# Retention states of two heads side by side with zeros, and earlier loads of three tensors

## The chip, the cores and the metric

One NeuronCore of a Trainium2 chip runs the whole program. The metric is the device time in microseconds (us) of one launch, median of the runs shown. TensorE (PE), VectorE (DVE), ScalarE (ACT), GpSimd (POOL) and the DMA queues of SyncE (SP), ACT and POOL are programmed by hand and meet at semaphores.

## The reference, cut to what matters

A two-layer decoder trunk, 1024 tokens by 1024 columns, float32. Layer 0 normalises x and multiplies it by one weight matrix of 3352 columns. Columns 0 to 2047 are queries, keys, values and a gate of 8 retention heads of width 64; columns 2048 to 2559 are the queries of 8 sparse-attention heads, and the rest their keys, values and gates. Retention works on chunks of 128 tokens:

```python
scores = einsum('bhcid,bhcjd->bhcij', q_c, k_c) * decay
y_intra = einsum('bhcij,bhcje->bhcie', scores, v_c)
chunk_kv = einsum('bhcjd,bhcje->cbhde', k_c * k_decay, v_c)
state = chunk_decay * state + kv          # one 64 x 64 state a head
y_inter = einsum('bhcid,cbhde->bhcie', q_c * q_decay, prev_states)
y = y_intra + y_inter                     # then a norm per head and a gate
```

Sparse attention, an output projection and a mixture of 32 experts (two of them per token) follow. Layer 1 has a gated convolution in place of the attention, and another mixture of experts. Each expert mixture adds two weighted rows per token to the residual stream.

## The kernel before, in words

`project_and_retain` computes the projection in 7 column blocks (six of 512 columns and one of 280), each for 8 tiles of 128 tokens. A product of one block and one tile is 24 matmuls (line 511): 8 slices of the depth, in three parts (high by high, high by low, low by high) that together give float32 accuracy. Each result goes through `stage` to the tensor `proj` in memory.

Retention is put in between. From block 3 (`GATE`) on, `step(b, t)` gives each chunk of 128 tokens four products in a row; after the first of them comes TURN, after the second SCORE, after the third WEIGH. So 8 chunks fill blocks 3 to 6, and the last WEIGH stands after the product of block 6, tile 6, with one product behind it.

- TURN (`turn_queries`, line 520): 8 transposes of queries and keys into `ps_a`.
- SCORE (`score`): the scores of each head, keys by queries with depth 64 (line 530), from partitions 0 to 63 for even heads (`a` = 0) and 64 to 127 for odd ones (`a` = 1), into two banks of `ps_s`; then each head's own key-value product (line 537) with 64 columns of output partitions, in the lower or upper half of `ps_kv`. A float32 matmul of these shapes is two instructions in the trace. The order is all four heads of `a` = 0, then all four of `a` = 1.
- WEIGH (`weigh`): for each head, scores by values with depth 128 (line 548), then decayed queries by `state` with depth 64 (line 550), accumulated in the same 64 columns of `ps_a`. The two kinds alternate, 16 matmuls in all.

The state of heads 2b and 2b+1 stands in partitions 0 to 63 and 64 to 127 of `state[:, b, :]`. ACT takes the result of WEIGH (lines 362 and 363), DVE updates `state` (lines 442 and 444) and norms and gates the rows in `norm_weighed`, POOL's queue stores them to `mixer`.

`rows_of_heads` is the next stage. Its block starts when every engine has ended the projection's. SP's queue then loads the queries of tile 0, all keys (two loads), two gains, `q_rows`, the queries of tiles 1 to 7, then the keys and values of the other branches. ACT and DVE wait for the keys, gains and `q_rows` together (`keys_loaded`), then work tile by tile. The queries `nq` lie where the projection's raw weights `raw` lay.

`experts` is the mixture. It ends with the last expert's output scattered to `slots` by a POOL DMA (line 1192). DVE sets `finished` when the last split of weights is done, and SP then loads tiles 0 to 3 of the residual rows for the stage that follows (`NextRows.load`, line 1069) while the last expert ends.

Two stages follow a mixture. `mix_and_conv` loads from `slots` two rows per token and tile (`ya`, line 1460, four tiles ahead), then residual rows of tiles 4 to 7, then the first convolution weights (line 1472, split by ACT at line 1514 and DVE at line 1568, in order between the tiles' work). `finish` loads `ya` of all 8 tiles and, after those of each tile from 4 on, its residual rows; DVE adds them up (line 2587), ACT's queue stores the output.

Of the kernel before, what the change touches and what calls it, by code (L numbers as in the profile page):

```python
# [16 lines left out]
ALU = mybir.AluOpType  # L17
# [173 lines left out]
def project_and_retain(nc, name, src, gain, w, width, out, ret_gain, con, y_out, cst, region):  # L191
# [8 lines left out]
    VALUES, GATE = 2, 3  # L200
    with Pool_(nc, name) as m:
# [20 lines left out]
        state = m.sb("state", [P, PAIRS, HD])  # L222
# [7 lines left out]
        ps_y = ps_a[:].rearrange("p a b n -> p a (b n)")  # L230
# [26 lines left out]
        with nc.Block(no_gpsimd_drain=True) as block:  # L257
            @block.sync
            def _(sp):
# [18 lines left out]
                for b in range(1, n_blocks):  # L278
                    for c in range(2):
                        load_weights(b, c)  # L280
                for s in range(4):
                    sp.wait_ge(stage_stored[s], 16 * n_blocks * (NT // 4))
# [38 lines left out]
            def _(act):  # L321
# [35 lines left out]
                def take_weighed(c):  # L357
                    act.wait_ge(y_ready, c + 1)
                    if c >= 2:
                        act.wait_ge(y_stored[c % 2], 16 * (c // 2))  # L360
                    halves = ps_y[:, :, 0:PAIRS * HD].rearrange("p a (b d) -> p a b d", d=HD)
                    act.activation(y_sq.rearrange("p (b a d) -> p a b d", a=2, d=HD), halves, ACT.Square)
                    act.activation(y[:, c % 2, :].rearrange("p (b a d) -> p a b d", a=2, d=HD), halves, ACT.Copy
                                   ).then_inc(y_taken, 1)
# [34 lines left out]
            def _(dve):  # L399
# [39 lines left out]
                def norm_weighed(c):  # L439
                    dve.wait_ge(kv_ready, c + 1)  # L440
                    dve.wait_ge(y_ready, c + 1)
                    dve.tensor_tensor(state[:], state[:], c_decay[:].unsqueeze(2).to_broadcast([P, PAIRS, HD]), ALU.mult)
                    dve.drain()
                    dve.tensor_tensor(state[:], state[:], ps_kv[:, 0:PAIRS, :], ALU.add).then_inc(state_ready, 1)
# [48 lines left out]
            def _(pe):  # L493
# [30 lines left out]
                def score(c):  # L524
                    pe.wait_ge(T_ready, c + 1)
                    pe.wait_ge(decayed, c)
                    for a in range(2):
                        at = slice(a * HD, (a + 1) * HD)
                        for b in range(PAIRS):
                            last = pe.matmul(ps_s[:, a, b, :], qkT[at, 1, b, :], qkT[at, 0, b, :], start=True, stop=True)  # L530
# [3 lines left out]
                    for a in range(2):  # L534
                        for b in range(PAIRS):
# [5 lines left out]
                def weigh(c):  # L541
                    pe.wait_ge(qd_ready, c + 1)
                    pe.wait_ge(decayed, c + 1)
                    for a in range(2):
                        at = slice(a * HD, (a + 1) * HD)
                        for b in range(PAIRS):
                            h = 2 * b + a
# [513 lines left out]
class NextRows:  # L1061
# [5 lines left out]
    def load(self, sp, tiles):  # L1067
        for t in tiles:
# [3 lines left out]
def experts(nc, name, data, lists, slots, most, ident, following):  # L1072
# [14 lines left out]
    with Pool_(nc, name) as m:  # L1087
# [59 lines left out]
        with nc.Block(no_gpsimd_drain=True) as block:  # L1147
            @block.sync
            def _(sp):
# [28 lines left out]
                following.load(sp, range(NT // 2))  # L1178
# [237 lines left out]
def mix_and_conv(nc, name, ahead_rows, slots, gates, gain, mix_out, cst, w, conv_w, conv_b, zT_hi, zT_lo, z_places, ahead, region):  # L1416
# [5 lines left out]
    with Pool_(nc, name) as m:  # L1422
# [31 lines left out]
        with nc.Block() as block:  # L1454
            @block.sync
            def _(sp):
# [13 lines left out]
                ahead_rows.load(sp, range(NT // 2, NT))  # L1470
# [207 lines left out]
def rows_of_heads(nc, name, proj, q_gain, k_gains, cst, con, keep, region):  # L1678
# [4 lines left out]
    with Pool_(nc, name) as m:  # L1683
        nq, kv, kvc = region.head_rows()
# [9 lines left out]
        rows_loaded, keys_loaded, pool_loaded, rest_loaded, mask_loaded = (  # L1694
            m.sems("rows_loaded", NT), m.sem("keys_loaded"), m.sem("pool_loaded"), m.sem("rest_loaded"), m.sem("mask_loaded"))
# [5 lines left out]
        with nc.Block() as block:  # L1701
            @block.sync
            def _(sp):
                def load_queries(t):
                    sp.dma_start(nq[:, t, :], proj[t * P:(t + 1) * P, C_NQ:C_KC]).then_inc(rows_loaded[t], 16)

                load_queries(0)
# [5 lines left out]
                for t in range(1, NT):  # L1713
                    load_queries(t)
# [764 lines left out]
def trunk(nc, a, con, out):  # L2479
# [3 lines left out]
    with ctx:  # L2483
# [10 lines left out]
        with Pool_(nc, "all", whole=True) as top:  # L2494
# [23 lines left out]

            with Pool_(nc, "in") as m:
# [111 lines left out]
```

## Time and profile before

| | us |
|---|---|
| median of 3 runs (2167.07 to 2169.96) | 2167.11 |
| profiled execution, its own time | 2173.11 |
| its span, first to last instruction | 2171.4 |
| projection with retention, until the next stage's first load | 418.0 |
| TensorE busy in the span | 1873.8 |

The profile is of one execution. The page lists costly groups of instructions; the trace answers finer questions: what one engine ran in a few microseconds (the timeline), how busy each engine was in a stretch and which clock TensorE was granted (windows), who waited for whom (waits). Matmuls overlap in the pipeline, so the time from one start to the next says more than the duration of one.

### The profile page before, as it was taken

The page shows a single profiled execution, that of the slowest core. Times are in us where ns is not written, and L with a number is a line of the kernel's source. Part 1 is how long each engine was busy: PE and PEld are TensorE (multiplying, and loading weights), DVE is VectorE, ACT ScalarE, POOL GpSimd, SP SyncE. Part 2 cuts the span into 40 slices and gives each one's busy share as a digit, 9 for nine tenths or more (in the row PEclk, how much of TensorE's full clock was granted, in tenths as well). Part 3 has the DMA queues.
Part 4 walks back from the last instruction along what each step waited for, and adds up shares of the span by engine and source line. Part 5 has one row for each costly group of instructions (what it writes and reads, how often), then busy time and mean ns, then how long its engine had stood idle before and what let it go on. Part 6 is the DMA issues. An engine that isn't in the chain of part 4 may idle for free. (4 is left out here: it accounts for less than half of the span.)

```text
span 2171.4 us, 25604 instructions
## 1 busy us (share of the span) xinstructions
PE 1873.8 (86%) x9608; PEld 1548.8 (71%) x9608; DVE 1223.7 (56%) x1566; ACT 865.5 (40%) x928; POOL 317.4 (15%) x258
## 2 busy tenths in 40 slices
PE   8999999655789999986999992799999959999980
PEld 7888888645577788865888772688887847888760
DVE  5223322366555544565999883633324557999873
ACT  4111221231233333234888882311112126888860
POOL 0000000000110000111443420000000112434420
PEclk9999889685799999987999996899999978999995
DMA  5333212340200003455999966521124348999947
GB/s 199 127 117 107 99 57 78 117 95 1 78 1 1 1 1 104 167 190 230 362 381 372 367 269 224 173 58 50 39 65 164 135 178 325 381 381 372 373 161 296
DMA packets 145297, 374.40 MB, mean 172 GB/s; under 512 B 40078, under 2 KB 75150, under 8 KB 120446
## 3 DMA queue, kind: packets, MB, share of 16 engines
q1 hardware_dynamic: 113542, 309.54, 38.9%
q0 software_dynamic: 22432, 45.53, 5.8%
q10 hardware_dynamic: 9216, 17.93, 2.2%
q8 instruction: 63, 1.03, 0.2%
q14 instruction: 44, 0.36, 0.1%
HBM read 331.38 MB, written 75.10 MB: 187 GB/s over the span
## 5 line engine op out<-in xcount | busy, mean ns | idle before, releaser
L1242 PE MATMUL ex_ps_h<-even_split 128*128 128x512 f32 x768 | 195.9, 406 | 9.2 <-DVE even_split L1356 9.0
L1242 PE MATMUL ex_ps_h<-odd_split 128*128 128x512 f32 x768 | 196.0, 406 | 8.9 <-DVE odd_split L1356 8.5
L511 PE MATMUL in_ps<-in_w_hi,in_xT_hi 128*128 128x512 f32 (+1 forms) x448 | 179.1, 400 | 1.7 <-DVE in_xT_lo L416 1.7
L1242 PEld LDWEIGHTS ex_ps_h<-even_split 128*128 128x128 f32 x768 | 142.5, 192 | 48.7 <-DVE even_split L1356 14.9
L1242 PEld LDWEIGHTS ex_ps_h<-odd_split 128*128 128x128 f32 x768 | 142.5, 192 | 48.4 <-DVE odd_split L1356 15.3
L511 PE MATMUL in_ps<-in_w_lo,in_xT_hi 128*128 128x512 f32 (+1 forms) x448 | 175.0, 391 | 0.0
L511 PE MATMUL in_ps<-in_w_hi,in_xT_lo 128*128 128x512 f32 (+1 forms) x448 | 174.3, 389 | 0.0
L1630 PE MATMUL conv_ps<-conv_xT_hi,conv_w_hi 128*128 128x512 f32 x384 | 150.4, 392 | 0.9 <-DVE conv_w_lo L1568 0.9
L1630 PE MATMUL conv_ps<-conv_xT_lo,conv_w_hi 128*128 128x512 f32 x384 | 149.8, 390 | 0.0
L1630 PE MATMUL conv_ps<-conv_xT_hi,conv_w_lo 128*128 128x512 f32 x384 | 149.7, 390 | 0.0
L2333 ACT ACTIVATE att_prob<-att_ps_s 128x512 f32<-128x512 f32 x114 | 67.9, 597 | 175.3 <-PE att_ps_s L2271 175.1
L423 DVE COPY in_stage<-in_ps 128x512 f32<-128x512 f32 (+1 forms) x56 | 36.7, 656 | 176.9 <-PE in_ps L511 176.9
L2285 PE MATMUL att_ps_o<-mix_v,att_prob 128*128 128x128 f32 x912 | 125.9, 284 | 0.3 <-DVE even_attended L2393 0.3
L2285 PEld LDWEIGHTS att_ps_o<-mix_v,att_prob 128*128 128x128 f32 x912 | 122.4, 201 | 4.6 <-ACT att_prob L2333 0.7
L2361 DVE TENSOR_REDUCE att_low<-att_ps_m 128x2 f32<-128x768 f32 (+7 forms) x80 | 71.8, 916 | 68.7 <-PE att_ps_m L2236 67.0
L511 PEld LDWEIGHTS in_ps<-in_w_hi,in_xT_hi 128*128 128x128 f32 x448 | 89.3, 199 | 19.0 <-DVE in_xT_lo L416 2.1
L511 PEld LDWEIGHTS in_ps<-in_w_hi,in_xT_lo 128*128 128x128 f32 x448 | 89.0, 199 | 16.3
L511 PEld LDWEIGHTS in_ps<-in_w_lo,in_xT_hi 128*128 128x128 f32 x448 | 89.5, 200 | 15.3
L1263 PE MATMUL ex_ps_y<-even_split,ex_h_hi 128*128 128x512 f32 x256 | 83.6, 408 | 5.4 <-DVE ex_h_lo L1370 5.4
L1263 PE MATMUL ex_ps_y<-odd_split,ex_h_hi 128*128 128x512 f32 x256 | 83.5, 408 | 5.4 <-DVE ex_h_lo L1370 5.4
L1630 PEld LDWEIGHTS conv_ps<-conv_xT_hi,conv_w_hi 128*128 128x128 f32 x384 | 72.4, 189 | 16.3 <-DVE conv_w_lo L1568 1.3
L990 PE MATMUL out_ps_o<-even_split,even_x_hi 128*128 128x512 f32 x256 | 81.6, 400 | 2.5 <-DVE even_x_lo L925 2.5
(343 smaller groups left out, 4060.9 us busy)
## 6 DMA issues: line engine op xcount, KB each, us to landing
all_region<-in_moe_w_gate SPq DMA_DIRECT2D x16, 1024.0 KB
all_region<-in_moe_w_up SPq DMA_DIRECT2D x16, 1024.0 KB
all_region<-in_moe_w_down SPq DMA_DIRECT2D x16, 1024.0 KB
experts_w_gu<-in_moe_w_gate SPq DMA_DIRECT2D x16, 1024.0 KB
experts_w_gu<-in_moe_w_up SPq DMA_DIRECT2D x16, 1024.0 KB
experts_w_d<-in_moe_w_down SPq DMA_DIRECT2D x16, 1024.0 KB, 15.0
all_region<-in_ev_w_in SPq DMA_DIRECT2D x12, 1024.0 KB, 7.5
proj<-in_stage ACTq DMA_DIRECT2D x48, 256.0 KB, 2.0
```

The lines of the kernel that those rows point to most:

```text
L423: dve.tensor_copy(stage[:, q % 4, 0:n], ps[:, q % BANKS, 0:n]).then_inc(staged, 1)
L511: last = pe.matmul(ps[:, q % BANKS, 0:n], a[:, k, at], w_part[:, b % 2, k, 0:n], start=(k == 0 and j == 0), stop=(k == KT - 1 and j == 2))
L990: last = pe.matmul(ps_o[:, t % 2, cols], a[:, k, :], w_part[:, b, k, :], start=(k == 0 and j == 0), stop=(k == KT - 1 and j == 2))
L1242: last = pe.matmul(ps_h[:, u % 2, :], a[:, u % 2, k, :], w[:, k, :], start=(k == 0 and j == 0), stop=(k == KT - 1 and j == 2))
L1263: last = pe.matmul(ps_y[:, at], a[:, u % 2, k, :], w[:, k, at], start=(k == 0 and j == 0), stop=(k == DE // P - 1 and j == 2))
L1630: last = pe.matmul(ps[:, j, at], w_part[:, j, k, :], x_part[:, k, at], start=(k == 0 and q == 0), stop=(k == KT - 1 and q == 2))
L2285: last = pe.matmul(ps_o[:, b, h * P:(h + 1) * P], prob[:, c % 4, h * P:(h + 1) * P], keep.v_all[:, v_at:v_at + P], start=(j == first_tile( ...
L2333: act.activation(prob[:, c % 4, :], ps_s[:, c % 2, :], ACT.Exp).then_inc(exped, 1)
L2361: dve.tensor_reduce(low[:, n % 2, b, hs[0]:hs[-1] + 1], src, X, ALU.max, negate=True).then_inc(reduced, 1)
```

## The change

The state is kept as `[P, PAIRS, 2, HD]`: for a pair of heads b, partitions 0 to 63 hold the even head's state in columns 0 to 63 and zeros in 64 to 127, partitions 64 to 127 zeros and then the odd head's state. One product of depth 128 and 128 columns then gives both heads' second term. WEIGH does its 8 products of scores and values first, then 4 of these, all in one bank. DVE updates the two halves apart. SCORE's loops are turned round, so that even and odd heads alternate. The sparse heads' queries are loaded by SP's queue in the projection, once their rows are in memory and the last raw weights are split. Residual rows of all 8 tiles are loaded when the experts' last split is done.

```diff
-        state = m.sb("state", [P, PAIRS, HD])
+        state = m.sb("state", [P, PAIRS, 2, HD])
-        ps_y = ps_a[:].rearrange("p a b n -> p a (b n)")
+        ps_y = ps_a[:, 0, :, :].rearrange("p b n -> p (b n)")
...
+                for c in range(2):
+                    sp.wait_ge(lo_ready[c], n_blocks)
+                for t in range(NT):
+                    in_memory(sp, QUERIES, t)
+                    ahead.load_queries(sp, t)
...
-                    halves = ps_y[:, :, 0:PAIRS * HD].rearrange("p a (b d) -> p a b d", d=HD)
-                    act.activation(y_sq.rearrange("p (b a d) -> p a b d", a=2, d=HD), halves, ACT.Square)
-                    act.activation(y[:, c % 2, :].rearrange("p (b a d) -> p a b d", a=2, d=HD), halves, ACT.Copy
-                                   ).then_inc(y_taken, 1)
+                    act.activation(y_sq, ps_y, ACT.Square)
+                    act.activation(y[:, c % 2, :], ps_y, ACT.Copy).then_inc(y_taken, 1)
...
-                    dve.tensor_tensor(state[:], state[:], c_decay[:].unsqueeze(2).to_broadcast([P, PAIRS, HD]), ALU.mult)
-                    dve.drain()
-                    dve.tensor_tensor(state[:], state[:], ps_kv[:, 0:PAIRS, :], ALU.add).then_inc(state_ready, 1)
+                    halves = [(slice(a * HD, (a + 1) * HD), a) for a in range(2)]
+                    for at, a in halves:
+                        dve.tensor_tensor(state[at, :, a, :], state[at, :, a, :],
+                                          c_decay[at, :].unsqueeze(2).to_broadcast([HD, PAIRS, HD]), ALU.mult)
+                    dve.drain()
+                    for at, a in halves:
+                        last = dve.tensor_tensor(state[at, :, a, :], state[at, :, a, :], ps_kv[at, 0:PAIRS, :], ALU.add)
+                    last.then_inc(state_ready, 1)
...
-                    for a in range(2):
-                        at = slice(a * HD, (a + 1) * HD)
-                        for b in range(PAIRS):
+                    for b in range(PAIRS):
+                        for a in range(2):
+                            at = slice(a * HD, (a + 1) * HD)
                             last = pe.matmul(ps_s[:, a, b, :], qkT[at, 1, b, :], qkT[at, 0, b, :], start=True, stop=True)
...
-                    for a in range(2):
-                        for b in range(PAIRS):
+                    for b in range(PAIRS):
+                        for a in range(2):
                             h = 2 * b + a
                             last = pe.matmul(ps_kv[a * HD:(a + 1) * HD, b, :], kd[:, h * HD:(h + 1) * HD],
...
-                            pe.matmul(ps_y[:, a, b * HD:(b + 1) * HD], scores[:, a, b, :],
-                                      qkv[:, c % 2, 2 * RET_W + h * HD:2 * RET_W + (h + 1) * HD], start=True, stop=False)
-                            last = pe.matmul(ps_y[:, a, b * HD:(b + 1) * HD], qdT[at, b, :], state[at, b, :],
-                                             start=False, stop=True)
+                    for h in range(RH):
+                        pe.matmul(ps_y[:, h * HD:(h + 1) * HD], scores[:, h % 2, h // 2, :],
+                                  qkv[:, c % 2, 2 * RET_W + h * HD:2 * RET_W + (h + 1) * HD],
+                                  start=(h == 0), stop=False, skip_group_check=True)
+                    for b in range(PAIRS):
+                        last = pe.matmul(ps_y[:, b * P:(b + 1) * P], qdT[:, b, :],
+                                         state[:, b, :, :].rearrange("p a d -> p (a d)"),
+                                         start=False, stop=(b == PAIRS - 1), skip_group_check=True)
...
-                following.load(sp, range(NT // 2))
+                following.load(sp)
...
-                ahead_rows.load(sp, range(NT // 2, NT))
...
+class HeadRows:
+    def load_queries(self, sp, t):
+        sp.dma_start(self.nq[:, t, :], self.proj[t * P:(t + 1) * P, C_NQ:C_KC]).then_inc(self.loaded[t], 16)
...
-                load_queries(0)
...
-                for t in range(1, NT):
-                    load_queries(t)
...
-                    if t >= NT // 2:
-                        ahead_rows.load(sp, [t])
```

## Rows read from the trace of the kernel before

**Rows 1.** The page: TensorE's granted clock in 40 slices of the span, tenths.

```profile
PEclk9999889685799999987999996899999978999995
```

**Rows 2.** Windows, one chunk of retention each; busy us (instructions), then clock and DMA.

```profile
164.90:199.18 34.28, 34.28 (x172) 28.14 (x169) 13.39 (x18) 5.61 (x7) 2.69 (x5) 0.90 0.44 146
...
368.07:392.72 24.65, 24.65 (x172) 22.92 (x169) 7.96 (x15) 5.61 (x7) 0.54 (x1) 0.86 0.10 35
```

**Rows 3.** Timeline of TensorE's matmuls in the first chunk: start, us, what.

```profile
164.10 1.03 PE L520 MATMUL in_ps_a<-all_ident,all_region 128*128 128x128 f32 x8
...
170.52 1.71 PE L530 MATMUL in_ps_s<-in_xn 64*128 64x128 f32 x16
172.16 0.97 PE L537 MATMUL in_ps_kv<-all_region,in_xin 128*64 128x64 f32 x16
173.05 0.50 PE L511 MATMUL in_ps<-in_w_hi,in_xT_hi 128*128 128x512 f32 x1
...
178.63 0.33 PE L548 MATMUL in_ps_a<-all_region,in_xin 128*128 128x64 f32 x2
178.89 0.43 PE L550 MATMUL in_ps_a<-in_state,in_xn 64*128 64x64 f32 x2
179.25 0.43 PE L548 MATMUL in_ps_a<-all_region,in_xin 128*128 128x64 f32 x2
...
182.90 0.69 PE L548 MATMUL in_ps_a<-all_region,in_xin 128*128 128x64 f32 x2
...
185.37 0.79 PE L511 MATMUL in_ps<-in_w_hi,in_xT_hi 128*128 128x512 f32 x1
```

**Rows 4.** Windows in SCORE, TensorE alone: busy us (matmuls in flight), clock.

```profile
170.88:170.92 0.04, 0.04 (x3) 1.00 0.00 0
...
171.44:171.48 0.04, 0.04 (x6) 1.00 0.00 0
```

**Rows 5.** Windows on line 1904 (first) and line 1997, both TensorE: busy, clock.

```profile
483.30:488.00 4.70, 4.62 (x42) 4.43 (x40) 1.00 0.00 0
...
510.00:520.00 10.00, 9.34 (x45) 9.73 (x44) 0.50 0.01 2
```

**Rows 6.** Timeline from the last WEIGH to the next stage, all engines.

```profile
401.67 0.33 PE L548 MATMUL in_ps_a<-all_region,in_xin 128*128 128x64 f32 x2
...
409.25 0.60 PE L511 MATMUL in_ps<-in_w_hi,in_xT_hi 128*128 128x280 f32 x1
...
409.43 0.43 DVE L442 TENSOR_TENSOR in_state<-in_state,in_c_decay 128x256 f32<-128x256 f32 x1 [7.11 <-PE in_ps_a L550]
...
415.65 0.33 ACTq L344 DMA_DIRECT2D proj<-in_stage  x1
418.00 0.34 SPq L1705 DMA_DIRECT2D all_region<-proj  x1
```

**Rows 7.** Waits in `rows_of_heads`: us in total, times, longest.

```profile
ACT heads_n_sq L1754 <- DMA heads_q_rows<-con_q_rows: 15.7, 1, 15.7
```

**Rows 8.** The end: timeline of the last scatter and `finish`, two windows, a wait.

```profile
2113.25 1.76 SPq L1069 DMA_DIRECT2D all_region<-stream  x4
...
2120.30 0.97 POOL L1192 DMA_INDIRECT slots<-ex_y,odd_idx  x1 [9.96 <-ACT ex_y L1317]
2127.60 5.56 SPq L2577 DMA_DIRECT2D end_ya<-slots  x10
...
2120.40:2123.60 3.20, 0.00 (x0) 0.00 (x0) 0.00 (x0) 0.00 (x0) 0.87 (x1) 0.68 0.19 68
...
2149.40:2164.50 15.10, 0.00 (x0) 0.00 (x0) 7.70 (x7) 0.00 (x0) 0.00 (x0) 0.50 1.01 410
...
DVE all_region L2587 <- DMA all_region<-stream: 10.9, 4, 3.7
```

**Rows 9.** Waits at the start of `mix_and_conv`: us in total, times, longest.

```profile
DVE all_region L1547 <- DMA odd_zT_lo_again<-slots: 7.9, 2, 4.7
ACT conv_w_hi L1514 <- DMA odd_zT_hi_again<-in_od_w_in: 4.9, 1, 4.9
```

More of the change, by code:

```diff
@@ L188, in load, with project_and_retain @@
             sp.dma_start(self.raw[b][:, at, :], self.w_k[:, at, b * COLS:(b + 1) * COLS]).then_inc(self.loaded[2 * b + c], 16)
-def project_and_retain(nc, name, src, gain, w, width, out, ret_gain, con, y_out, cst, region):
+def project_and_retain(nc, name, src, gain, w, width, out, ret_gain, con, y_out, cst, region, ahead):
     n_blocks = -(-width // COLS)
@@ L199, in project_and_retain @@
     PAIRS = RH // 2
-    VALUES, GATE = 2, 3
+    VALUES, GATE, QUERIES = 2, 3, 4
     with Pool_(nc, name) as m:
@@ L543, in weigh @@
                     pe.wait_ge(decayed, c + 1)
[L544 to L547, printed above, removed]
-                            pe.matmul(ps_y[:, a, b * HD:(b + 1) * HD], scores[:, a, b, :],
-                                      qkv[:, c % 2, 2 * RET_W + h * HD:2 * RET_W + (h + 1) * HD], start=True, stop=False)
-                            last = pe.matmul(ps_y[:, a, b * HD:(b + 1) * HD], qdT[at, b, :], state[at, b, :],
-                                             start=False, stop=True)
+                    for h in range(RH):
[6 more added lines that the diff above has]
+                                         start=False, stop=(b == PAIRS - 1), skip_group_check=True)
                     last.then_inc(y_ready, 1)
@@ L1065, in __init__, with load @@
         self.src, self.rows, self.loaded = src, region.stream_rows(), m.sems(name, NT)
-    def load(self, sp, tiles):
-        for t in tiles:
+    def load(self, sp):
+        for t in range(NT):
             sp.dma_start(self.rows[:, t, :], self.src[t * P:(t + 1) * P, :]).then_inc(self.loaded[t], 16)
@@ L1675, with __init__, rows_of_heads @@
 KEY_EXT = EXT + 2 * R
-def rows_of_heads(nc, name, proj, q_gain, k_gains, cst, con, keep, region):
+class HeadRows:
+    def __init__(self, m, proj, region):
+        self.proj, self.loaded = proj, m.sems("head_rows_loaded", NT)
+        self.nq, self.kv, self.kvc = region.head_rows()
+    def load_queries(self, sp, t):
+        sp.dma_start(self.nq[:, t, :], self.proj[t * P:(t + 1) * P, C_NQ:C_KC]).then_inc(self.loaded[t], 16)
+def rows_of_heads(nc, name, proj, q_gain, k_gains, cst, con, keep, ahead):
     NK = 2 * G
@@ L1683, in rows_of_heads @@
     with Pool_(nc, name) as m:
-        nq, kv, kvc = region.head_rows()
+        nq, kv, kvc = ahead.nq, ahead.kv, ahead.kvc
         gains = m.sb("gains", [P, 3, HD])
@@ L1693, in rows_of_heads @@
         ps_n = m.ps("ps_n", [P, 3, ROUND, P])
-        rows_loaded, keys_loaded, pool_loaded, rest_loaded, mask_loaded = (
-            m.sems("rows_loaded", NT), m.sem("keys_loaded"), m.sem("pool_loaded"), m.sem("rest_loaded"), m.sem("mask_loaded"))
+        rows_loaded = ahead.loaded
+        keys_loaded, pool_loaded, rest_loaded, mask_loaded = (
+            m.sem(n) for n in ("keys_loaded", "pool_loaded", "rest_loaded", "mask_loaded"))
         eps_ready, n_squared, n_summed, n_rooted, rows_added, n_ready = (
@@ L1703, in _ @@
             def _(sp):
-                def load_queries(t):
-                    sp.dma_start(nq[:, t, :], proj[t * P:(t + 1) * P, C_NQ:C_KC]).then_inc(rows_loaded[t], 16)
-                load_queries(0)
                 for j, (a, b) in enumerate(((C_KS, C_VS), (C_KW, C_VW))):
@@ L2517, in route @@
                                   data, lists, rows)
+            head_rows = HeadRows(top, proj, region)
             with Pool_(nc, "in") as m:
                 project_and_retain(nc, "in0", a["x"][0, :, :], a["mix_norm_g"][0, :], a["ev_w_in"][0, :, :], IN_W, proj,
-                                   a["ev_ret_norm_g"][0, :], con, mixer, cst, region)
+                                   a["ev_ret_norm_g"][0, :], con, mixer, cst, region, head_rows)
             with Pool_(nc, "even") as held:
@@ L2531, in trunk @@
                             rows_of_heads(nc, "heads", proj, a["ev_q_norm_g"][0, :], a["ev_k_norm_g"][0, :, :], cst, con, keep,
-                                          region)
+                                          head_rows)
                             sparse_prepare(nc, "prep", a["ev_q_norm_g"][0, :], a["ev_k_norm_g"][0, :, :], a["ev_cmp_pe"][0, :, :, :],
```

## The prediction

> **What bounds the kernel now.** I read the page first, for the clock. TensorE runs at 2.4 GHz when the granted clock is 1.0 and at 1.2 GHz when it is 0.5; a slice that shows 8 or 9 tenths mixes the two levels [rows 1]. The projection fills the first 418 us. Windows cut along the chunks show TensorE busy for all of each, at a mean clock of 0.90, falling to 0.86 where the products are narrow, while DVE has 13.4 us of work in 34.3, ACT 5.6 and POOL 2.7 [rows 2]. So in this stage every microsecond of TensorE is one of the kernel, until the last WEIGH; DVE, ACT and DMA follow.
>
> The timeline shows what retention costs between the products [rows 3]. TURN's eight transposes are short. SCORE runs from 170.52 to 173.05, 2.53 us. WEIGH runs from 178.63 to 185.37, 6.74 us, for 32 instructions. At 182.90 a pair's duration jumps from 0.43 to 0.69 us: the clock has gone to half, inside WEIGH and nowhere else in the chunk. The chunk's mean of 0.90 says for how long: 0.1 of 34.28 us is lost, so 6.8 us ran at half clock. The last two products of this chunk carry the rest of it. The next TURN comes 34.28 us after 164.10, at 198.38, so those two take 13.01 us, where one at full clock takes 5.58 (173.05 to 178.63). The narrower chunk shows the same loss (0.14 of 24.65 us is 3.45), so it is one such stretch a chunk.
>
> Why is WEIGH slow before the fall? The two kinds alternate every 0.36 us, two instructions each (178.89 to 179.25), 0.18 us an instruction. A stream of one kind with 128 columns of weights goes faster: 42 instructions of line 1904 in 4.70 us, 0.112 each, at full clock [rows 5]; two of them would take 0.22. So each change between 128 and 64 rows of depth costs about 0.14 us, and there are 16 of them in a WEIGH.
>
> **The change, part by part.**
>
> WEIGH. 32 instructions in 16 alternating pairs become 24 of one depth: 16 with 64 columns and 8 with 128, all with 128 columns of weights. At 0.112 [rows 5] that is 2.7 us, and there is no change of depth left within it or at its edges. Per chunk 6.74 − 2.7 = 4.0 us go. If the clock then does not fall, the two products behind it take 11.1 instead of 13.0, another 1.9. That makes 5.9 us for each of 7 chunks, 41.3 us. The bounds of an instruction are 0.055 (line 537's 16 in 0.89 us, with half the weight columns) and 0.21 (line 1997, 45 in 9.34 us at half clock [rows 5]): WEIGH between 1.3 and 5.0 us. I take 0.112, because the shape of line 1904 is the one nearest, 128 by 128. The zeros cost nothing more: the product has 128 columns for two heads, where it had 64 for each.
>
> The last chunk. Its WEIGH took 7.58 us, 401.67 to 409.25 [rows 6], and takes 2.7: 4.9 less. From 409.25 to 418.00 are 8.75 us more, 6.4 until the last store's issue at 415.65 and 2.35 for it to land. At full clock the last product would end some 2 us sooner. But in DVE's order the whole norm of the weighed rows, which begins with line 442 at 409.43, stands ahead of the copy of that product, and it gets longer by two state operations of 0.43 [rows 6]. So between nothing and 2 us go here; I take 0.4, near the lower end, since the norm's chain over DVE and ACT sets the copy from now on. The last chunk gives 5.3 in all.
>
> DVE. Two more state operations a chunk, at most 0.43 us each, since the elements a partition are as before. In the other chunks they hide under the products: DVE is idle over 20 us of 34 [rows 2]. If that cover were gone they would cost 7 us over the eight chunks. ACT reads the same 512 elements in one stretch: nothing. The longer clear of `state` lies before the first x tile is in.
>
> SCORE. Even and odd heads now alternate. In the old order one half alone keeps 3 matmuls in flight, and at 171.44 there are 6 [rows 4]: the second half started before the first was done, so the two halves do run side by side. Eight instructions of one half at 0.11 are 0.9 us, plus an edge of 0.2, against 1.64 (170.52 to 172.16), so 0.5 less if both start together. Line 537 likewise: 16 in 0.89 us, one half 0.44 and an edge of 0.15, so 0.3 less. That is 0.8 a chunk, 6.4 us. From below the bound is nothing gained, from above 8 × 1.2 = 10 (half of 2.53 each); the loss that it could bring is a rival below. The Trainium skill, page "TensorEngine Tiling (Array Packing)", section "Key Properties", says that a change of tiling mode drains the engine, but not a change of tile, and that different tiles can load weights and multiply in parallel. By that rule WEIGH loses its pauses and SCORE gains none; the trace agrees with the first part by its 0.14 us and with the second by the six in flight.
>
> Queries ahead. Eight loads of 256 KB move to SP's queue in the projection, behind the last weights. Nothing of the stage stands behind them on that queue but waits for stores that come later anyway, and the DMA engines are busy for 0.44 of the time or less in these chunks [rows 2]. In `rows_of_heads` ACT starts after a wait that `q_rows` ended [rows 7]. One query load stood ahead of it (0.34 us of issue [rows 6], 256 KB) and seven right behind it shared the engines. The bounds are that issue alone and all 2.1 MB at 410 GB/s [rows 8], 5.1 us; I take 1.5, near the lower one, because only one of the eight stood ahead. Later the stage goes by DVE and ACT tile by tile, so that other loads land sooner buys nothing.
>
> Residual rows, at the end. In `finish` DVE waited 10.9 us over four tiles for rows of the stream; from 2149.4 to 2164.5 the DMA engines moved 410 GB/s at full share [rows 8]. Four loads of 512 KB less are 2.1 MB, 5.2 us at that rate. They now go right behind the first four, which were issued from 2113.25 on. The scatter was issued at 2120.30 and moved 68 GB/s for 3.2 us, 0.2 MB, and the last stage began at 2127.60. Eight loads at 410 GB/s take 10.2 us, to about 2124: ahead of 2127.6, but across the scatter. I give 1 us back for it: 4.2, bounds 1 and 5.2. DVE's own work there, two operations of 1.3 us a tile, is 21 us, so DMA stays the limit.
>
> Residual rows, after the first mixture. The same four loads stood ahead of the first convolution weights, for which ACT waited 4.9 us, with the next tile's squares behind it in ACT's order and the split behind it in DVE's [rows 9]. 2.1 MB less ahead of the weights is 5.1 us and takes the 4.9 away. Less 1 for the scatter and 0.4 because DVE comes to its part of the weights later than ACT: 3.5. Bounds are 1, and 6 if some of DVE's 7.9 us for the gathered rows [rows 9] goes too.
>
> **The sum.** 41.3 + 5.3 + 6.4 + 1.5 + 4.2 + 3.5 = 62.2 us. The profiled execution took 2173.11 (span 2171.4 and 1.7 around it), so the same would show 2110.9 for it. It lies 6.0 above the median of the runs; from 2167.11 the forecast is 2104.9, say 2105. A run tells differences from about 0.2%, 4.3 us, here.
>
> **Rivals.**
>
> The clock still falls in each WEIGH. For it: line 1997, 128 columns of weights by 64 columns, the shape of the new WEIGH's first 16 instructions, ran at 0.50 without a rise while TensorE was over 90% busy [rows 5]. Against it: those 16 are 1.8 us, the 8 behind them have line 1904's shape, which was at 1.0, and SCORE, 2.5 us long and about as light, shows no fall in any chunk. Price: 6.8 us at half clock lose 3.4, eight times 27: 2132. Chance 0.13.
>
> Alternating halves pause. If each of the 14 changes of half in SCORE costs the 0.14 us of a change of depth, that is 2.0 a chunk, 16 us, and the 6.4 are not gained: 2127. The six in flight speak against it. Chance 0.10.
>
> The same on the other side: this is also what could make the kernel slower. It decides when one of the 8 × 14 changes of half costs more than (62.2 − 6.4) / 112 = 0.50 us, three and a half times the pause in WEIGH. At 0.6 the time would be 2105 + 6.4 + 67 = 2179. Chance 0.02.
>
> The moved rows gain nothing: eight loads delay the last scatter, and the next stage starts as much later as it gets shorter. For it: the scatter's data has the engines to itself today [rows 8]. Against: it is only 0.2 MB. Price 7.7: 2113. Chance 0.12. The Trainium skill, page "DMA: Bandwidth & Descriptors", section "Issuing engines are not separate DMA queues", says that transfers of all engines' queues interleave on the same 16; by that the scatter shares rather than waits its turn, and this rival would cost about 1 to 2 us instead. No row here has the two together.
>
> The forecast itself, with its terms within their bounds, has 0.60, and 0.03 is left to what I do not see.
>
> **How the numbers follow.** The likeliest case's own range: 2096 if WEIGH is 2.4 us, SCORE gains 10 and the row loads all of their 5 to 6; 2114 if SCORE gains nothing and the heads and row loads little. The pause in SCORE reaches 2127 and the moved rows 2113. Leaving out most of the clock's case at 2132, the slow case and a little below, the range is 2094 to 2130. Slower by over 0.2% needs the 0.50 us pause or something unseen: 0.02. Within 0.2%: 0.02. Faster: 0.96.
>
> **What would show it.** In the profile after: one chunk in 34.3 − 5.9 − 0.8 = 27.6 us; no 0.50 stretch in blocks 3 to 6, a mean clock of 1.00 there; WEIGH near 2.7 us with no pauses; SCORE near 1.7; the next stage's first load near 365; the first squares of the heads about 1.5 us sooner after it; no wait of DVE for rows of the stream in `finish`, and its length down from 44 to 39 us. The prediction is wrong if the clock row still shows 0.9 in the chunks, if instructions of WEIGH stay at 0.18 us because what slows them is the accumulation into columns just written and not the change of depth, or if the stages behind the mixtures start late.

## The result and the profile after

The changed kernel takes 2116.94 us (median of 4 runs, 2111.78 to 2119.13), against 2168.45 (4 runs, 2167.07 to 2169.96) for the one before on the same chip: a ratio of 0.9759, 95% interval 0.9739 to 0.9779, 51.5 us in the medians. Three later measurements of the same two kernels gave 59.1, 59.0 and 57.2 us. The forecast was 2105, in a range of 2094 to 2130, with a change of 62.2.

The profiled execution took 2111.78 us (span 2110.2), 61.3 less than the profiled one of before. It is the fastest of its four; the other three have spans of 2114.7 to 2117.5 at a mean granted clock of 0.913 to 0.916 where it has 0.919. The profiled one of before was slower than all four of its runs in that comparison. So the stage comparisons below flatter the change, by some 10 us in all against the first medians and by 2 to 4 against the later ones, and the medians are the better measure of the whole.

The clock row of the page after, 40 slices of the span:

```profile
PEclk9999999767899999969999995999999969999995
```

The nearly eight slices of the projection [rows 1] are now nearly seven, and the two 8s among their 9s are gone. A slice does not show a stretch of 6.8 us, so I cut windows along the chunks again; one chunk to a line, busy us (instructions) of PE, PEld, DVE, ACT, POOL, then clock, DMA share and GB/s. The last line is the wide middle of the narrow last block.

```profile
163.03:190.33 27.30, 27.30 (x162) 22.97 (x161) 14.24 (x18) 5.62 (x7) 2.70 (x5) 1.00 0.55 183
190.33:217.63 27.30, 27.30 (x162) 22.97 (x161) 9.83 (x16) 9.33 (x9) 1.61 (x3) 1.00 0.26 87
320.00:344.00 24.00, 24.00 (x206) 23.40 (x205) 11.93 (x21) 6.20 (x8) 1.62 (x3) 1.00 0.21 70
```

A chunk takes 27.30 us, where it took 34.28 at a clock of 0.90 [rows 2]. The clock is 1.00 throughout. TensorE is still busy for all of it, so it is still what bounds the stage. The timeline of TensorE in the first chunk:

```profile
163.03 1.03 PE L530 MATMUL in_ps_a<-all_ident,all_region 128*128 128x128 f32 x8
...
169.44 1.16 PE L540 MATMUL in_ps_s<-in_xn 64*128 64x128 f32 x16
170.54 0.69 PE L547 MATMUL in_ps_kv<-all_region,in_xin 128*64 128x64 f32 x16
171.15 0.50 PE L521 MATMUL in_ps<-in_w_hi,in_xT_hi 128*128 128x512 f32 x1
...
176.75 1.89 PE L556 MATMUL in_ps_a<-all_region,in_xin 128*128 128x64 f32 x16
178.48 1.11 PE L560 MATMUL in_ps_a<-in_state,in_xn 128*128 128x128 f32 x8
179.34 0.48 PE L521 MATMUL in_ps<-in_w_hi,in_xT_hi 128*128 128x512 f32 x1
...
351.23 1.89 PE L556 MATMUL in_ps_a<-all_region,in_xin 128*128 128x64 f32 x16
352.96 1.11 PE L560 MATMUL in_ps_a<-in_state,in_xn 128*128 128x128 f32 x8
353.83 0.37 PE L521 MATMUL in_ps<-in_w_hi,in_xT_hi 128*128 128x280 f32 x1
```

SCORE goes from 169.44 to 171.15, 1.71 us for 2.53 [rows 3]. WEIGH goes from 176.75 to 179.34, 2.59 us for 6.74, in two rows in place of sixteen pairs, because no idle time cuts them apart. The last chunk's WEIGH is the same, 2.60 for 7.58 [rows 6]. What follows it, all engines but TensorE:

```profile
359.41 0.45 DVE L428 COPY in_stage<-in_ps 128x280 f32<-128x280 f32 x1
359.68 0.55 POOL L321 DMA_DIRECT2D mixer<-in_y  x1 [17.18 <-DVE in_y L466]
359.89 0.33 ACTq L351 DMA_DIRECT2D proj<-in_stage  x1
363.53 1.00 SPq L1727 DMA_DIRECT2D all_region<-proj  x2
```

The copy now ends DVE's chain right behind the norm, as the prediction read it from the order. The two last stores are issued within 0.3 us of each other (1.5 apart before), and the stage ends 3.64 us after the last, for 2.35. From the end of the last WEIGH to the next stage are 9.7 us, for 8.75. All of the increase is behind the last store's issue: up to it are 6.06 us, for 6.40. In the thirteen profiles of kernels with the change or most of it, the stage ends 3.35 to 3.78 us after that issue.

The stage behind, and the two places where the rows of the stream moved:

```profile
372.91 0.63 ACT L1770 ACTIVATE heads_n_sq<-all_region 128x512 f32<-128x512 f32 x1 [15.30 <-DMA heads_q_rows<-con_q_rows]
...
1256.94 4.25 SPq L1080 DMA_DIRECT2D all_region<-stream  x8
...
1264.13 0.97 POOL L1203 DMA_INDIRECT slots<-ex_y,even_idx  x1 [10.09 <-ACT ex_y L1328]
1276.74 0.80 SPq L1471 DMA_DIRECT2D odd_zT_lo_again<-slots  x2
...
2052.53 6.79 SPq L1080 DMA_DIRECT2D all_region<-stream  x8
2059.71 0.98 POOL L1203 DMA_INDIRECT slots<-ex_y,odd_idx  x1 [10.08 <-ACT ex_y L1328]
2072.53 10.83 SPq L2594 DMA_DIRECT2D end_ya<-slots  x16
```

After the last scatter of the second mixture the kernel now waits 12.8 us for the last stage to begin, where it waited 7.3 [rows 8]; after the first mixture 12.6, where it was 9.25 (1321.62 to 1330.87). Windows from the issue to just before the first packet of the scatter, and from there to its last, by the trace's records of packets:

```profile
2059.80:2064.00 4.20, 0.00 (x0) 0.00 (x0) 0.00 (x0) 0.00 (x0) 0.89 (x1) 0.68 1.03 376
2064.10:2068.10 4.00, 0.00 (x0) 0.00 (x0) 0.00 (x0) 0.00 (x0) 0.00 (x0) 0.50 0.58 226
```

While the rows of the stream fill the engines (share 1.03), no packet of the scatter moves. Its first starts 4.4 us after the issue, where it took 1.5 before (2120.30 to 2121.84), and its packets spread over 4.0 us, where they took 1.6.

The stages against before; heads and the convolution each from its first load to the next stage's first:

| | before | after | difference | forecast |
|---|---|---|---|---|
| projection, to the first load of the next stage | 418.00 | 363.53 | −54.5 | −53.0 |
| heads | 44.2 | 41.9 | −2.3 | −1.5 |
| last scatter of the first mixture to the convolution | 9.25 | 12.6 | +3.4 | +1 |
| the convolution's stage | 314.8 | 311.1 | −3.7 | −4.5 |
| last scatter of the second mixture to `finish` | 7.3 | 12.8 | +5.5 | +1 |
| `finish`, to the end of the span | 43.8 | 37.7 | −6.1 | −5.2 |

They add up to −57.7 of the −61.2 between the spans; the other 3.5 lie in stages that the change does not touch. Of the 54.5, 1.1 stand ahead of the first chunk (its TURN starts at 163.03 for 164.10), where nothing was changed; the other profiles have that start anywhere from 162.8 to 164.2.

### The profile page after: what moved, and what is told of

It reads as the page before. It is cut to its first block and busy times, and to the rows that moved or that the text cites. A ratio compares the mean times of both kernels' runs of the same rounds, so it can differ in the third digit from the quotient of the medians.

```text
span 2110.2 us, 25493 instructions
## 1 busy us (share of the span) xinstructions
PE 1815.4 (86%) x9544; PEld 1504.2 (71%) x9544; DVE 1231.0 (58%) x1582; ACT 865.2 (41%) x928; POOL 317.4 (15%) x258
## 3 DMA queue, kind: packets, MB, share of 16 engines
q1 hardware_dynamic: 113542, 309.54, 39.9%
## 5 line engine op out<-in xcount | busy, mean ns | idle before, releaser
L521 PE MATMUL in_ps<-in_w_hi,in_xT_hi 128*128 128x512 f32 (+1 forms) x448 | 171.8, 384 | 1.7 <-DVE in_xT_lo L421 1.7
L521 PE MATMUL in_ps<-in_w_lo,in_xT_hi 128*128 128x512 f32 (+1 forms) x448 | 168.9, 377 | 0.0
L521 PE MATMUL in_ps<-in_w_hi,in_xT_lo 128*128 128x512 f32 (+1 forms) x448 | 168.8, 377 | 0.0
L521 PEld LDWEIGHTS in_ps<-in_w_hi,in_xT_hi 128*128 128x128 f32 x448 | 84.7, 189 | 17.1 <-DVE in_xT_lo L421 2.1
L521 PEld LDWEIGHTS in_ps<-in_w_hi,in_xT_lo 128*128 128x128 f32 x448 | 84.6, 189 | 15.3
L521 PEld LDWEIGHTS in_ps<-in_w_lo,in_xT_hi 128*128 128x128 f32 x448 | 84.7, 189 | 14.3
```

Of the source, the lines that this page charges most:

```text
L521: last = pe.matmul(ps[:, q % BANKS, 0:n], a[:, k, at], w_part[:, b % 2, k, 0:n], start=(k == 0 and j == 0), stop=(k == KT - 1 and j == 2))
```

## The experiments

Every kernel here computes all of the reference. The changed kernel itself ran again as the control three times, each time beside the kernel before and some of the others; "against the control" is against its median there. Timed differences under some 3 us are read together with a stage of the trace or not at all, since the control's own runs spread over 3 to 4 us.

**The controls.** The first of them:

> The changed kernel once more, to have it beside the next three on one chip. All theories: 2112 to 2119 us, as in its four runs so far.

It took 2111.81 (2111.18 to 2114.6) for 2170.95 before, a ratio of 0.9732 [0.9716, 0.9748]. The other two, 2113.7 for 2172.65 (0.9729 [0.9714, 0.9745]) and 2115.42 for 2172.6 (0.9735 [0.9716, 0.9753]), had these:

> The changed kernel again, beside the next three on one chip: 2111 to 2119 us.

> The changed kernel again, beside the next three on one chip: 2111 to 2119 us.

The last scatter was again followed by 12.5 and 11.7 us in the second of them, and the next stage's first load stood at 363.95, 364.45 and 364.24: the mechanisms of the table repeat. The first 51.5 us in the medians does not; all later ones lie at 57 to 59. What held that first set up stays open.

**WEIGH alone put back**, with the state still in two halves:

```
-                    for h in range(RH):
-                        pe.matmul(ps_y[:, h * HD:(h + 1) * HD], scores[:, h % 2, h // 2, :], ...)
-                    for b in range(PAIRS):
-                        last = pe.matmul(ps_y[:, b * P:(b + 1) * P], qdT[:, b, :], state[:, b, :, :] ...)
+                    for a in range(2):
+                        for b in range(PAIRS):
+                            pe.matmul(ps_y[:, a, b * HD:(b + 1) * HD], scores[:, a, b, :], ...)
+                            last = pe.matmul(ps_y[:, a, b * HD:(b + 1) * HD], qdT[at, b, :], state[at, b, a, :], ...)
```

> The changed kernel with WEIGH as it was: depth 128 and depth 64 alternate, head by head, into two banks; all else stays changed. Theory (WEIGH's shape gave 4.1 us a chunk by itself and 2 through the clock): WEIGH 6.4 to 7.2 us again, one stretch at half clock in each of the 8 chunks, about 47 us over the changed kernel, 2161 to 2166. Rival (SCORE's quicker order, or DVE's halves, kept the clock up): no fall of the clock, WEIGH 5.8 us, about 26 us over, 2143.

2158.51 (2152.55 to 2162.47), 46.7 us above the control. The timeline of its first WEIGH, and windows before the fall, behind it, and over the chunk:

```profile
177.88 0.43 PE L563 MATMUL in_ps_a<-in_state,in_xn 64*128 64x64 f32 x2
178.24 0.43 PE L561 MATMUL in_ps_a<-all_region,in_xin 128*128 128x64 f32 x2
...
181.39 0.69 PE L561 MATMUL in_ps_a<-all_region,in_xin 128*128 128x64 f32 x2
182.00 0.69 PE L563 MATMUL in_ps_a<-in_state,in_xn 64*128 64x64 f32 x2
```

```profile
176.89:180.78 3.89, 3.89 (x23) 3.15 (x21) 0.69 (x1) 0.00 (x0) 0.00 (x0) 1.00 1.00 323
181.39:185.00 3.61, 3.61 (x12) 2.95 (x12) 0.88 (x3) 1.04 (x2) 0.53 (x1) 0.50 0.43 159
163.50:197.00 33.50, 33.50 (x171) 27.38 (x170) 14.32 (x19) 5.61 (x7) 2.69 (x5) 0.90 0.47 149
```

The pauses and the stretch at half clock are back together: 0.36 us a pair at 1.00, 0.62 at 0.50, and a chunk of 33.5 us at 0.90. The next stage's first load comes at 408.56, 44.6 later than the control's. So WEIGH carries about four fifths of the gain. It does not say yet what about it.

**Is it the full depth, or the order?** Two kernels take one of the two away. The first keeps the zeros out of the products, each head with its own half of depth, but puts all products of one depth together:

```
+                    for b in range(PAIRS):
+                        for a in range(2):
+                            pe.matmul(ps_y[:, a, b * HD:(b + 1) * HD], scores[:, a, b, :], ... start=(b == 0), stop=False)
+                    for b in range(PAIRS):
+                        for a in range(2):
+                            at = slice(a * HD, (a + 1) * HD)
+                            last = pe.matmul(ps_y[:, a, b * HD:(b + 1) * HD], qdT[at, b, :], state[at, b, a, :], ...)
```

> The changed kernel with WEIGH grouped but without the zeros' product: first the 8 products of depth 128, then 8 of depth 64, even and odd heads alternating, into two banks. Theory (the pauses come from changes of depth, of which one is left, and two halves run side by side): 16 instructions at 0.112, a change of 0.15, 16 of the halves in 1.1: WEIGH 3.1 us against 2.6, no fall of the clock, 4 us over the changed kernel, 2121. Rival (the product of full depth is what matters): instructions of depth 64 stay at 0.18 us, WEIGH 4.7 or more, and the clock falls: 2117 + 8 x 4 = 2149.

The second has the full depth and the zeros, but alternates the two kinds, each head's second product adding to the columns just written, in 32 instructions:

```
                     for h in range(RH):
+                        b, at = h // 2, slice(h * HD, (h + 1) * HD)
                         pe.matmul(ps_y[:, at], scores[:, h % 2, b, :], ...)
+                        last = pe.matmul(ps_y[:, at], qdT[:, b, :], state[:, b, h % 2, :], ...)
```

> The changed kernel with WEIGH in the old alternating order but all at depth 128: after each head's product with the values comes its product with its own 64 columns of the padded state (zeros in the other half of the depth), accumulated into the columns just written. Theory (changes of depth make the pauses): 32 instructions at 0.112, WEIGH 3.6 us, 1 us a chunk more than the changed kernel, 2125; clock as likely up as not, since 64-column products are all that runs, and if it falls 20 us more. Rival (accumulating into columns just written makes the pauses): 0.18 us an instruction, WEIGH 5.8, the clock falls, 2155 or more.

The first took 2117.48 (2116.66 to 2118.58), the second 2119.81 (2118.3 to 2122.13): 5.7 and 8.0 above the control, where WEIGH as before costs 46.7. The WEIGH of the first:

```profile
177.96 1.89 PE L560 MATMUL in_ps_a<-all_region,in_xin 128*128 128x64 f32 x16
179.78 1.11 PE L566 MATMUL in_ps_a<-in_state,in_xn 64*128 64x64 f32 x16
180.82 0.50 PE L523 MATMUL in_ps<-in_w_hi,in_xT_hi 128*128 128x512 f32 x1
```

and of the second:

```profile
177.01 0.33 PE L557 MATMUL in_ps_a<-all_region,in_xin 128*128 128x64 f32 x2
177.18 0.39 PE L560 MATMUL in_ps_a<-in_state,in_xn 128*128 128x64 f32 x2
177.40 0.39 PE L557 MATMUL in_ps_a<-all_region,in_xin 128*128 128x64 f32 x2
```

Grouped, with one change of depth, WEIGH takes 2.86 us and a chunk 27.60: the product of full depth saves 0.27 a WEIGH, 2.2 over eight, and the stage ends 3.1 later than the control's. Alternating at one depth, pairs follow each other every 0.22 us (0.11 an instruction), with no pause although each adds to what the one ahead of it wrote; WEIGH takes 3.5 us and a chunk 28.2, eight more instructions at 0.11. In neither does the clock fall in any chunk. So the pauses come with the change of depth, not with the accumulation. (`start` at each head, which the old WEIGH has and this one lacks, is no rival either: every product of SCORE has it, and its 16 instructions of scores take 1.10 us.) Taking the pauses away is enough for the clock. The zeros are one way to do it; an order would have done nearly as well: 3.1 us later at the stage's end, 5.7 in the medians, of 46.7.

**Is it the pauses or the length?** A WEIGH without pauses might keep the clock only because it is short. This kernel does WEIGH twice over, alternating at full depth; the second pass begins with `start` at head 0 again and writes over the first:

```
-                    for h in range(RH):
+                    for h in [*range(RH), *range(RH)]:
```

> WEIGH in the alternating order at full depth, done twice over (the first pass is overwritten): 64 instructions at 0.112, 7.2 us, as long as the old WEIGH but without a change of depth. Theory (the pauses of 0.14 us, with TensorE doing little in a stretch of 6 us, let the clock fall, not the length of the light stretch): the clock stays up in all chunks; 4.6 us a chunk over the changed kernel, 37 in all, 2150. Rival (a stretch of 6 us of small products is enough): the clock falls in most chunks, 16 to 27 us more, 2166 to 2177.

2149.16 (2146.48 to 2149.16), 33.7 above the control beside it. Windows on its first WEIGH and its first chunk:

```profile
176.54:183.60 7.06, 7.06 (x65) 7.06 (x64) 0.69 (x1) 0.00 (x0) 0.00 (x0) 1.00 0.83 289
162.00:193.77 31.77, 31.77 (x202) 27.43 (x201) 14.23 (x18) 6.05 (x8) 2.70 (x5) 1.00 0.49 157
```

For 7.06 us TensorE does nothing but products of 64 columns (64 instructions), longer than the old WEIGH's 6.74, and the clock stays at 1.00, here and in every other chunk. The difference to the fall is the weight loads: busy for all of this stretch, and for 3.15 of 3.89 us in the stretch just before the fall with the old WEIGH. Half of the old instructions also used half the depth. Which of the two, the gaps or the lighter load, brings the fall, these runs don't part.

**SCORE in its old order:**

```
-                    for b in range(PAIRS):
-                        for a in range(2):
+                    for a in range(2):
+                        for b in range(PAIRS):
```

at both places.

> The changed kernel with SCORE's old order, even heads first and then odd. Theory (halves of the array run side by side, alternating lets both start together): SCORE 2.5 us instead of 1.7 in each chunk, 6.5 us over the changed kernel; the clock stays up in the chunks. Rival (SCORE's time was gained elsewhere, or a longer light stretch lets the clock fall): SCORE stays 1.7, or 20 us over.

2122.16 (2116.41 to 2123.2), 8.5 above the control. The timeline of its first SCORE:

```profile
169.78 1.71 PE L540 MATMUL in_ps_s<-in_xn 64*128 64x128 f32 x16
171.42 0.97 PE L547 MATMUL in_ps_kv<-all_region,in_xin 128*64 128x64 f32 x16
172.31 0.50 PE L521 MATMUL in_ps<-in_w_hi,in_xT_hi 128*128 128x512 f32 x1
```

2.53 us as before, against 1.71 in the changed order: 0.82 a chunk, and the next stage starts 6.0 us later. The clock stays up. The other 2.5 us of the timed difference lie within the spread.

**The queries loaded in the heads' own stage again**, one at its head and seven behind the first rows:

```
-                    in_memory(sp, QUERIES, t)
-                    ahead.load_queries(sp, t)
...
+                ahead.load_queries(sp, 0)
...
+                for t in range(1, NT):
+                    ahead.load_queries(sp, t)
```

> The changed kernel with the sparse heads' queries loaded in their own stage again, tile 0 ahead of the keys, the others behind q_rows. Theory (one load ahead of the keys and some sharing): the first squares 1 to 2 us later after the stage's start, 1.5 us over the changed kernel. Rival (hidden anyway, DVE and ACT set the stage): the same as the changed kernel.

2118.22 (2116.63 to 2120.17), 2.8 above the control; the heads' stage takes 45.8 us for 42.9. Its first squares stand here:

```profile
374.41 0.63 ACT L1768 ACTIVATE heads_n_sq<-all_region 128x512 f32<-128x512 f32 x1 [16.10 <-DMA heads_q_rows<-con_q_rows]
```

10.2 us after the stage's first load at 364.23, against 9.0 to 9.5 in the controls. This 1 us at the first wait is what the traces show; it is outside the 9.0 to 9.5 of all twelve profiles with the queries ahead. The rest of the 2.9 is not shown to be the queries': the stage's length goes from 40.6 to 44.3 us over those twelve, with the same loads in all of them.

**The rows of the stream put back**, four ahead of each last scatter and four in the stage behind:

```
-                following.load(sp)
+                following.load(sp, range(NT // 2))
...
+                ahead_rows.load(sp, range(NT // 2, NT))
...
+                    if t >= NT // 2:
+                        ahead_rows.load(sp, [t])
```

> The changed kernel with the residual rows of tiles 4 to 7 loaded where they were, in the stage behind each mixture. Theory (the eight loads hold up the last scatter; the two ends gained 0.3 and 0.6 us in the traces, not 3.5 and 4.2): from the last scatter's issue to the next stage 9.2 and 7.3 us instead of 12.6 and 12.8, the stages behind as much longer; 1 us over the changed kernel, within what can be told. Rival (the forecast's terms hold and something else grew): 7 to 8 us over.

2116.3 (2113.89 to 2118.12), 2.6 above the control. The last scatters are followed by 8.4 and 7.1 us instead of 12.5 and 11.7; the convolution takes 314.1 for 310.8 and `finish` 44.6 for 37.6. The wait for rows in `finish`, of which the control has none, is back:

```profile
DVE all_region L2605 <- DMA end_ya<-slots: 21.4, 2, 20.5
DVE all_region L2605 <- DMA all_region<-stream: 11.2, 4, 4.0
```

Both stages do get shorter by the move, by 3.3 and 7.1 us, 10.4 together. 8.7 of that is given back at the two scatters. By that 1.7 us are left; like the timed 2.6 they lie within the spread.

**The second four rows only after the scatter:**

```
-                following.load(sp)
+                following.load(sp, range(NT // 2))
+                sp.wait_ge(all_scattered, 1)
+                following.load(sp, range(NT // 2, NT))
```

with a count by GpSimd behind its last scatter.

> The changed kernel, but SP loads the rows of tiles 4 to 7 only when GpSimd has seen the last scatter land, still in the mixture's block. Theory (the scatter shares the engines with the loads in flight and is held up by them): scatter to next stage 9.2 and 7.3 us again, and the four loads run in the 4 to 5 us from the scatter's end to the next stage, and a little beyond; 3 and 5 us gained at the two ends, 2117 - 8 = 2109, or 8 under the changed kernel of this call. Rival (the delay has nothing to do with the scatter but with eight loads issued in this block, their queue or the end of the block): no gain, same as the changed kernel.

2113.58 (2111.48 to 2115.8), the same as the control; the 8 us that the theory forecast are not there. The scatters are followed by 10.3 and 9.1 us, halfway. The timeline shows where the other half went:

```profile
2058.23 15.65 SPq L1080 DMA_DIRECT2D all_region<-stream  x8
2065.22 0.97 POOL L1205 DMA_INDIRECT slots<-ex_y,odd_idx  x1 [9.89 <-ACT ex_y L1331]
2074.36 12.41 SPq L2597 DMA_DIRECT2D end_ya<-slots  x16
```

The scatter was freed: its first packet starts 1.5 us after the issue and its last ends at 3.0. The queue was not: SP, which has to reach the end of the mixture's block too, waits until 2072.1 and issues the last four until 2073.88, 8.7 us after the scatter's issue. `finish`, with those loads now beside its own, takes 39.9 us for 37.6.

**All eight rows earlier**, before the scatter and out of its way. The buffers that they go to are free after the split of the fourth expert from the end, which DVE now says by a count of its own; before, SP waited until DVE was wholly done. The cut shows SP's side for the last round, without the counts of the rounds ahead of it:

```
-                sp.wait_ge(finished, 1)
+                sp.wait_ge(released, 1)
...
                 following.load(sp)
+                sp.wait_ge(finished, 1)
```

> The changed kernel, but SP loads all eight tiles of residual rows as soon as the first weight buffer and the first two row buffers are free, after the split of the fourth expert from the end, instead of after the last split. Theory (the last scatter is held up by the loads in flight when it is issued): no load is in flight then, so from scatter to next stage 7 to 8.5 us, as with the old loads, or a little less, while the stages behind keep their shorter times: 3.5 and 5 us gained, 8 under the changed kernel of this call. Rival (the loads now hold up the last experts' weights or scatters instead): the mixtures grow by as much, no gain.

2105.78 (2102.3 to 2108.74), 9.6 below the control and 0.9694 [0.9674, 0.9713] of the kernel before: the fastest kernel here. The rows are now loaded from 1233.3 and 2025.6 on, 35 us ahead of the scatters. Its timeline at the two scatters, and a window from the first packet of the second:

```profile
1268.54 0.97 POOL L1209 DMA_INDIRECT slots<-ex_y,even_idx  x1 [10.08 <-ACT ex_y L1334]
1276.75 0.80 SPq L1478 DMA_DIRECT2D odd_zT_lo_again<-slots  x2
...
2060.88 0.97 POOL L1209 DMA_INDIRECT slots<-ex_y,odd_idx  x1 [9.89 <-ACT ex_y L1334]
2068.38 8.86 SPq L2601 DMA_DIRECT2D end_ya<-slots  x16
```

```profile
2062.40:2064.50 2.10, 0.00 (x0) 0.00 (x0) 0.00 (x0) 0.00 (x0) 0.00 (x0) 0.50 0.26 94
```

The scatter is alone on the engines again (94 GB/s), the stages start 8.2 and 7.5 us after it, and both stages keep their short times (309.4 and 37.1). Against the 12.4 and 12.4 us of the control beside it that is 9.0 us less, what the loads had cost at the two scatters.

## Why the prediction was right, and where it was off

**The clock** and **WEIGH**: right, and the largest part. Forecast 27.6 us a chunk, a WEIGH of 2.7 and no stretch at 0.50; measured 27.30, 2.59 and none. That a change of depth makes the pause, at 0.14 us, was worked out from a difference of two rows and could have been the accumulation; alternating products of one depth showed 0.11 an instruction, so it was the depth. The rule of the Trainium skill, page "TensorEngine Tiling (Array Packing)", section "Key Properties", by which a change of tiling mode drains the engine, agrees with that. What the prediction did not see is that the zeros, which the change is named for, are worth little of the 47: 0.27 us a WEIGH, 3.1 us at the stage's end. And one reading of the rival on the clock was wrong: line 1997 does not have the shape of the new WEIGH's first 16 instructions; it has as many columns, but 81 rows of depth where they have 128. The rival was rightly doubted, but the row was weaker evidence for it than the prediction says.

**The last chunk**: its WEIGH gave 5.0, as forecast (4.9), but the way from there to the next stage became 0.95 longer where I had 0.4 shorter, so the term gave 4.0 instead of 5.3. What was forecast of that way came: the norm, with two operations more, now sets the copy, and the last store is issued 0.34 us sooner after the WEIGH. What the sum lacks is the landing. It left the 2.35 us as they were; they became 3.64. The store of `y` and the last store of the projection are now issued together, which may be why; no run parts them.

**SCORE**: 0.82 a chunk for 0.8, with the stage 6.0 us shorter for 6.4. The two halves run side by side more fully when they alternate, and a change of half costs no pause: the rival that it does, at 2127, falls, and with it the one on the slower side, whose 0.50 us a change would have made SCORE longer and not shorter.

**Queries ahead**: 2.3 in the profiled stages, 2.9 when undone, for 1.5. The first wait gave 0.4 to 1.0 of that. The rest lies within the stage's own spread of 3.7 us, so the runs neither confirm nor refute that other loads landing sooner buy nothing later in the stage. The term is right in sign; its size stays open between 0.4 and 2.9.

**The residual rows**: here a step failed in size, twice. Both gains were about right: the convolution 3.7 and `finish` 6.1 shorter, or 3.3 and 7.1 when undone, against 4.5 and 5.2 before the scatter's share. The step that failed is "I give 1 us back for it". The scatter's delay was 3.4 and 5.5 us, and the two terms that the sum holds at 7.7 were worth 0.3 and 0.6 between the profiled executions and, together, 1.7 by the stages and 2.6 in the medians when undone. What happened is the rival that the moved rows gain nothing, which had 0.12. I argued from the scatter's 0.2 MB. That size was the same in every kernel; the delay went with the bytes in flight when it was issued. The Trainium skill, page "DMA: Bandwidth & Descriptors", section "Issuing engines are not separate DMA queues", has the transfers of all issuing engines run on the same 16 DMA engines and interleave. The trace agrees that they share the engines, but not that the scatter shared from its start: its first packet moved only after 4.4 us at full share of the others. The cost of 1 to 2 us was my own estimate from that rule, and the measurement contradicts it.

**The sum**: 62.2 forecast. The experiments that undo one part give 46.7 + 8.5 + 2.8 + 2.6 = 60.6, and the three later comparisons 57 to 59. The scatter took about 5 us from the forecast and the last chunk 1.3; the queries, as undone, gave 1 more than it, and the chunks 0.3 each. That the sum still comes near the later comparisons is in part luck: these errors have both signs. The first measured median, 2116.94, is 11.9 above the forecast; some 7 of those are the distance between that set of runs and the later ones, which no trace here explains.

## What to carry to other kernels

Where small products of two depths alternate on TensorE, group them by depth before anything else: it cost nothing here and took both the pauses and the half clock away, and padding with zeros added little to it. Where a stage waits for a last small transfer, ask how many bytes stand in flight when it is issued, not how large it is; prefetches for the next stage belong well ahead of it, and if only a coarse wait holds them there, split the wait. And undo each part of a change by itself: two of its parts nearly cancelled here, and the time of the whole would never have shown it.

## What the runs showed of the hardware

Products of 64 columns do not by themselves bring the clock down: 64 instructions of them in 7.06 us ran at 1.00 throughout. Line 1997, with as many columns but only 81 rows of depth, stood at 0.50 without a rise from its first to its last instruction; part of that is in [rows 5], and this is its view:

```profile
L1997 PE MATMUL prepS_ps<-mix_kcT,mix_qT x128: 314/421/421, 493.7 to 522.9; 81*128 81x64 f32 x128
```

Whether the depth or the level at which it began makes that difference, no run shows. Changes between 128 and 64 rows of depth cost 0.14 us each; changes between the two halves at the same 64 rows cost nothing that the trace shows (16 instructions in 1.10 us alternating, 1.64 without [rows 3]). And a scatter issued by GpSimd behind eight loads of 512 KB on SP's queue moved nothing for 4.4 us (1.5 with four such loads ahead of it, or with none in flight), so that the next stage started 3.4 to 5.5 us later.
